# Two of four channel chunks of a 31-tap depthwise convolution computed on TensorE with diagonal weight matrices

## The reference, cut to what matters

```python
def conformer_conv(u, conv_w, conv_b, ln_g, ln_b):
    h = u[..., :D_CONV] * jax.nn.sigmoid(u[..., D_CONV:])            # D_CONV = 512 channels
    h = lax.conv_general_dilated(                                     # depthwise, causal, 31 taps
        h, conv_w[:, None, :], window_strides=(1,), padding=[(CONV_WIDTH - 1, 0)],
        dimension_numbers=("NWC", "WIO", "NWC"), feature_group_count=D_CONV) + conv_b
    return jax.nn.silu(layer_norm(h, ln_g, ln_b))

y_conv = conformer_conv(p[..., :2 * D_CONV], ...)
y_rwkv, v_first = rwkv7_mix(p[..., 2 * D_CONV:], ...)    # a recurrence over the tokens, 8 heads of 64
y = jnp.concatenate([y_conv, y_rwkv], axis=-1) @ w_out
```

## Time and profile before

| | |
|---|---|
| three runs | 1853.69, 1849.98, 1853.31 us; median 1853.31 us |
| the profiled execution, first to last instruction | 1854.3 us (no other time of its own is given) |
| busy: PE / DVE / ACT / POOL | 1675.9 / 1033.2 / 818.9 / 75.5 us |
| mean granted TensorE clock | 0.933 of full speed |
| the stretch of this case | inversion 132.96 to 193.0 us, scan 193.0 to 266.2 us |

### The profile page before, as it was taken

How to read it: one execution, slowest core, us unless ns; L and a number is a source line. 1 busy time by engine, 2 the same in 40 slices (tenths; PEclk the granted TensorE clock), 3 DMA queues, 4 the chain that set the end, 5 groups by cost and what they waited for, 6 DMA issues and landing times.

```text
span 1854.3 us, 29063 instructions
## 1 busy us (share of the span) xinstructions
PE 1675.9 (90%) x11870; PEld 1535.3 (83%) x11870; DVE 1033.2 (56%) x1405; ACT 818.9 (44%) x1211; POOL 75.5 (4%) x84
## 2 busy tenths in 40 slices
PE   6776878997999799999778999999989998899998
PEld 6675657887999699987568999899977998779998
DVE  4868446545554555455855545555443784555554
ACT  5330024545444544444355444544444566554443
POOL 1200000000000000000300000000000004300000
PEclk9887558998999899999899999999989999899999
DMA  6230002523555355544214555455534441145452
GB/s 231 92 115 2 1 23 83 191 104 145 183 183 186 127 187 189 187 162 181 91 69 159 182 181 186 154 187 190 186 118 150 169 182 46 44 162 182 181 183 111
DMA packets 37047, 263.61 MB, mean 142 GB/s; under 512 B 4192, under 2 KB 4320, under 8 KB 5728
## 3 DMA queue, kind: packets, MB, share of 16 engines
q1 hardware_dynamic: 35680, 257.97, 38.4%
q0 software_dynamic: 704, 2.62, 0.4%
q10 hardware_dynamic: 576, 1.78, 0.3%
HBM read 261.30 MB, written 1.05 MB: 141 GB/s over the span
## 4 chain that ended last, share of the span: by engine, by line
PE 83%; DVE 10%; ACT 4%; issue 1%; DMA 1%; POOL 0%; DVEq 0%; POOLq 0%; ACTq 0%
PE PS L374 24%; PE PS L375 24%; PE PS L376 24%; DVE w_lo L1194 2%; PE PS L555 1%; PE PS L368 1%; PE PS L790 1%; DVE arena L1448 1%; PE PS L767 1%; PE PS L456 1%; PE PS L480 1%; DVE x_normed L1211 1%; PE PS L594 1%; DMA x_resid<-x 1%; PE PS L619 1%
## 5 line engine op out<-in xcount | busy, mean ns | idle before, releaser
L1194 DVE TENSOR_TENSOR w_lo<-raw_weights,w_hi 128x1024 fp32r<-128x1024 f32 x488 | 601.9, 1239 | 551.8 <-ACT w_hi L836 551.2
L836 ACT ACTIVATE w_hi<-raw_weights 128x1024 fp32r<-128x1024 f32 x488 | 514.6, 1057 | 579.3 <-PE PS L376 557.1
L374 PE MATMUL PS<-h_hi,w_hi 128*128 128x256 f32 x2320 | 665.0, 287 | 19.8 <-DVE w_lo L1194 13.7
L375 PE MATMUL PS<-h_lo,w_hi 128*128 128x256 f32 x2320 | 662.2, 285 | 0.0
L376 PE MATMUL PS<-h_hi,w_lo 128*128 128x256 f32 x2320 | 661.8, 285 | 0.0
L374 PEld LDWEIGHTS PS<-h_hi,w_hi 128*128 128x128 f32 x2320 | 451.0, 194 | 23.9 <-DVE w_lo L1194 14.3
L375 PEld LDWEIGHTS PS<-h_lo,w_hi 128*128 128x128 f32 x2320 | 450.9, 194 | 2.2 <-issue 0.5
L376 PEld LDWEIGHTS PS<-h_hi,w_lo 128*128 128x128 f32 x2320 | 450.3, 194 | 0.0
L374 PE MATMUL PS<-w_hi,g_hi 128*128 128x512 f32 x440 | 172.0, 391 | 0.0
L375 PE MATMUL PS<-w_lo,g_hi 128*128 128x512 f32 x440 | 171.9, 391 | 0.0
L374 PE MATMUL PS<-w_hi,h_hi 128*128 128x512 f32 x352 | 145.2, 413 | 29.4 <-DVE w_lo L1194 14.5
(11 more groups left out here) (290 smaller groups left out, 1389.7 us busy)
## 6 DMA issues: line engine op xcount, KB each, us to landing
raw_weights<-W SPq DMA_DIRECT2D x244, 1024.0 KB, 4.8
post_gain<-post_gains POOLq DMA_DIRECT2D x3, 512.0 KB, 4.2
x_resid<-x SPq DMA_DIRECT2D x1, 1024.0 KB, 9.4
arena<-mem POOLq DMA_DIRECT2D x1, 1024.0 KB, 5.3
out<-x_resid SPq DMA_DIRECT2D x1, 1024.0 KB, 4.0
ptab<-cols ACTq DMA_DIRECT2D x1, 857.0 KB, 8.7
ctab<-consts ACTq DMA_DIRECT2D x1, 704.0 KB, 5.7
rtab<-rows ACTq DMA_DIRECT2D x1, 176.0 KB, 11.5
```

The costliest lines, as they stand in the source:

```text
L374: mm(out, lhs[0], rhs[0], start=start, stop=False)
L375: mm(out, lhs[0], rhs[1], start=False, stop=False)
L836: A(w_hi[:, n % H, :], raw[:, n % (2 * R), :], ACT.Copy).then_inc(S.hi_ready, 1)
L1194: v.tensor_tensor(w_lo[:, n % H, :], raw[:, n % (2 * R), :], w_hi[:, n % H, :].bitcast(F32), ALU.subtract).then_inc(S.lo_ready, 1)
```

## The change

The convolution's chunks 0 and 1 stay on DVE: `taps` has 62 entries now, and each call of `tap_steps` does half of what it did (4 per half level, 6, 6 and the last 10 in the scan). DVE waits for its own result after every two taps. Chunks 2 and 3 go to PE: a tap is a matmul whose stationary operand is a 128x128 diagonal matrix with the tap's 128 weights and whose moving operand is the shifted `glu`, and all 31 taps of a chunk accumulate in half of PSUM bank 7. The 62 taps are cut into 16 groups of four (the last has two). ACT makes the diagonals, 128x128 each, as identity x weight, into two buffers of four (one in the second half of `conv`, one new). PE takes one group ahead of each of its waits of levels 0 to 3 (four groups a level), and ACT makes the diagonals behind its Q copies. After level 4 ACT moves bank 7 with the bias to `conv`. `conv_ready` now counts two.

```diff
--- before.py
+++ after.py
@@ -143,6 +143,7 @@
         r_f, k_f, v_f = Q_r[:, 0:1024], Q_r[:, 1024:2048], Q_r[:, 2048:3072]
         conv = region(o, 1024); o += 1024
         usig = conv
+        diag = [ap.rearrange("p (s n) -> p s n", s=4) for ap in (conv[:, 512:1024], sb("diagonals", 512)[:])]
         MEM = region(o, 2048).rearrange("p (t d) -> p t d", t=TT)
         glu = region(o, 1024); o += 1024
         decay = region(o, 1024); o += 1024
@@ -225,7 +226,7 @@
                  "consts_loaded sin_ready qk_normed kk_std rows_loaded diff_ready kk_used scan_done "
                  "invP_ready rk_ready g_sum qk_evac qk_sq qk_ms qk_std qk_roped qkT_done qkT_ready v_ready "
                  "ang_ready trig_ready dt_done dt_abs dt_exp dt_ln aneg dta_ready acs_done acs_ready decay2_done "
-                 "conv4_ready xbc_ready z_ready2 sT_done sT_ready g_cb g_lt g_w g_y g_st g_stready g_xdt g_xdec "
+                 "diag_ready conv_mm conv4_ready xbc_ready z_ready2 sT_done sT_ready g_cb g_lt g_w g_y g_st g_stready g_xdt g_xdec "
                  "g_yev ys_sq ys_ms ys_std ysn_ready ysT_done ysT_ready").split()
         S = namedtuple("Signals", NAMES)(*[sem(n) for n in NAMES])
         loaded = [sem(f"loaded{r}") for r in range(R)]
@@ -234,6 +235,9 @@
         def done(eng, name, slot, i=0):
 
             eng.wait_ge(S.half_done, LOOP * i + 2 * (FIRST[name] + slot) + 2)
+
+        PE_TAPS = [(c, back) for c in (2, 3) for back in range(31)]
+        TAP_GROUPS = [PE_TAPS[i:i + 4] for i in range(0, len(PE_TAPS), 4)]
 
         def ffn_half(f, kind, b):
 
@@ -279,7 +283,7 @@
                     pool.wait_ge(S.pin_ready, 11)
                     tt(glu, glu, usig, ALU.mult).then_inc(S.glu_ready, 1)
 
-                    pool.wait_ge(S.conv_ready, 1)
+                    pool.wait_ge(S.conv_ready, 2)
                     pool.wait_ge(S.inv_ready, 12)
                     pool.dma_start(MEM, mem_in.rearrange("(t p) d -> p t d", p=P)).then_inc(S.mem_loaded, 16)
 
@@ -567,11 +571,25 @@
                 gram(6, Bt, Rt, t).then_inc(S.gram_done, 1)
             pe.wait_ge(S.gram_ready, 2)
 
+            def conv_taps(k):
+
+                if k >= len(TAP_GROUPS):
+                    return
+                if k == 0:
+                    pe.wait_ge(S.glu_ready, 1)
+                pe.wait_ge(S.diag_ready, k + 1)
+                for i, (c, back) in enumerate(TAP_GROUPS[k]):
+                    last = mm(PS[:, 7, (c - 2) * T + back:(c - 1) * T], diag[k % 2][:, i, :],
+                              glu[:, c * T:(c + 1) * T - back], start=back == 0, stop=back == 30)
+                last.then_inc(S.conv_mm, 1)
+
             for lv in range(5):
                 for t in range(TT):
+                    conv_taps(4 * lv + t)
                     pe.wait_ge(S.inv_ready, 2 * lv + t + 1)
                     blockmul(3 * t, Loffs[t], XiTs[t], t).then_inc(S.invq_done, 1)
                 for t in range(TT):
+                    conv_taps(4 * lv + 2 + t)
                     pe.wait_ge(S.invq_ready, 2 * lv + t + 1)
                     last = blockmul(3 * t + 1, Xis[t], Qis[t], t)
                     if lv < 4:
@@ -622,7 +640,7 @@
                                   stop=g == 0 or h % 2 == 1)
                 last.then_inc(S.yc_done, 1)
 
-            pe.wait_ge(S.conv_ready, 1)
+            pe.wait_ge(S.conv_ready, 2)
             for t in range(TT):
                 for c in range(4):
                     last = nc.tensor.transpose(PS[:, 4 + t, c * P:(c + 1) * P],
@@ -988,10 +1006,29 @@
 
             act.wait_ge(S.ang_ready, 1)
             A(trig, trig, ACT.Sin).then_inc(S.trig_ready, 1)
+            def diagonals(k):
+
+                if k >= len(TAP_GROUPS):
+                    return
+                if k >= 2:
+                    act.wait_ge(S.conv_mm, k - 1)
+                for i, (c, back) in enumerate(TAP_GROUPS[k]):
+                    last = A(diag[k % 2][:, i, :], ident, ACT.Copy, scale=pc("conv_w", (30 - back) * 4 + c))
+                last.then_inc(S.diag_ready, 1)
+
+            act.wait_ge(S.glu_ready, 1)
+            diagonals(0)
+            diagonals(1)
             for lv in range(5):
                 for t in range(TT):
                     act.wait_ge(S.invq_done, 2 * lv + t + 1)
                     A(Qis[t], PS[:, 3 * t, :], ACT.Copy).then_inc(S.invq_ready, 1)
+                    for k in ((4 * lv + 2,), (4 * lv + 3, 4 * lv + 4, 4 * lv + 5))[t]:
+                        diagonals(k)
+            act.wait_ge(S.conv_mm, len(TAP_GROUPS))
+            for c in (2, 3):
+                last = A(conv[:, c * T:(c + 1) * T], PS[:, 7, (c - 2) * T:(c - 1) * T], ACT.Identity, bias=pc("conv_b", c))
+            last.then_inc(S.conv_ready, 1)
             for g in range(NCK):
                 t, cp = g // 2, 64 * (g % 2)
                 act.wait_ge(S.ru_done, g + 1)
@@ -1431,11 +1468,11 @@
 
             h8 = lambda ap: ap.rearrange("p (h t) -> p h t", h=8)
             b8 = lambda m: m.unsqueeze(1).broadcast_to([P, 8, 64])
-            taps = [(back, c) for back in range(31) for c in range(4)]
+            taps = [(back, c) for back in range(31) for c in range(2)]
 
             def tap_steps(n):
 
-                if len(taps) == 124:
+                if len(taps) == 62:
                     dve.wait_ge(S.glu_ready, 1)
                 for _ in range(min(n, len(taps))):
                     back, c = taps.pop(0)
@@ -1447,7 +1484,7 @@
                         late = conv[:, c * T + back:(c + 1) * T]
                         last_ = v.scalar_tensor_tensor(late, glu[:, c * T:(c + 1) * T - back], weight, late,
                                                        ALU.mult, ALU.add)
-                    if c == 3 and taps:
+                    if c == 1 and taps:
                         step(last_)
                     elif not taps:
                         last_.then_inc(S.conv_ready, 1)
@@ -1479,7 +1516,7 @@
                         v.tensor_tensor(Xi, Xi, PS[:, b + 2, :], ALU.add)
                         last = v.tensor_tensor(h8(Loff), h8(NL), b8(cn("off", (lv + 2) * 64, 64)), ALU.mult)
                     last.then_inc(S.inv_ready, 1)
-                    tap_steps(8)
+                    tap_steps(4)
                     if lv == 0 and t == 0:
 
                         for c in range(4):
@@ -1492,7 +1529,7 @@
                     last = v.scalar_tensor_tensor(Zn[:, g % 2, c, :], PS[:, 3, c * P:(c + 1) * P], Pc[:, c * 4 + g, 64:65],
                                                   cn("pair"), ALU.mult, ALU.mult)
                 last.then_inc(S.z_ready, 1)
-                tap_steps(12 if g < NCK - 2 else len(taps))
+                tap_steps(6 if g < NCK - 2 else len(taps))
 
             y8 = lambda t: Y[:, t, :].rearrange("p (h d) -> p h d", h=8)
             b8h = lambda s_, t: s_[:, 8 * t:8 * t + 8].unsqueeze(2).broadcast_to([P, 8, 64])
```

## The result

| | before | changed kernel |
|---|---|---|
| 13 runs each on the same chip, median | 1853.48 us (1849.98 to 1855.62) | 1857.21 us (1855.17 to 1861.39) |
| profiled execution, span | 1854.3 us | 1856.1 us |
| mean granted clock | 0.933 | 0.941 |

The ratio is 1.0021, with a 95% interval of 1.0013 to 1.0030: slower by 3.7 us, where +2.2 us was forecast. VectorE gave up 62 instructions, TensorE took on 62 matmuls, and the kernel lost a little. Two later executions, one of e2 (2157.61 us) and one of the kernel before (2145.54 us), ran at a mean granted clock of 0.73 and 0.72 and are left out of every median.

A forecast was written before the change was run, and what follows sets the result against it. TensorE carries 83% of the chain, which alternates with VectorE in the inversion; TensorE would bound levels 0 to 3. Scan start +2.9, first scan product -0.9, `w_out` +0.2 on 1853.3 give 1855.5 us, range 1847.5 to 1862.5.

The forecast's parts named there:

- The taps behind t=0: Inversion: VectorE's taps here stand on the path; halving them saves 1.65 us a level, at most 8.2 us over five.
- PE becomes the bound of levels 0 to 3: Inversion: 8.1 us of new TensorE work a level does not fit into 4 us of idle time; VectorE waits.
- 13.5 us a level: TensorE's work in an inversion level: four groups 6.5, eight shape changes 1.6, six block products 5.4 us.
- Full clock from 136.5 on: Inversion: without idle time TensorE's granted clock stays at 1.00 from about 136.5 us, with 1.7 us either way.
- ScalarE hidden: Inversion: the 62 diagonals, at most 1.5 us a group of four, fit ScalarE's idle time and cost nothing.
- The stages: Inversion: VectorE starts later by 4.1 us after level 0, 7.3 after level 3, 4.5 after level 4; scan 2.9.
- The sum: Whole kernel: scan starts 2.9 us later, its first product saves 0.9, `w_out` adds 0.2: 2.2 us over the median.
- The later clock rise in `w_out`: Behind the scan: a later start shifts when the clock rises, a few tenths either way; 0.2 us added.
- Groups in the idle time: Rival, inversion: a group with its changes costs 1.3 instead of 2.0 us, a level 10.8 us; 1846 us, chance 5%.
- dearer groups: Rival, inversion: shape changes of 0.30 us, or late diagonals costing 1 us a level; 1858.5 to 1862 us, chance 12%.
- a half clock in the inversion: Rival: TensorE's clock stays at half there, a level takes 25 us; 1904 us, chance 2%.
- The clock through the scan: Rival: the scan starts and stays at full clock, its matmuls run twice as fast, saving 27 us; 1829 us, chance 8%.

The follow-up runs named there:

- e2: Changed kernel with all 124 taps on VectorE as well as all 16 groups on TensorE, their result thrown away: 1862.51 us, ratio 1.0051.
- e1: Changed kernel without TensorE's groups and ScalarE's diagonals, so half the taps are left out altogether: 1843.56 us, ratio 0.9951.
- e3: Changed kernel with the same 16 groups placed in pairs, four changes of array shape a level instead of eight: 1854.83 us, ratio 1.0008.
- e7: Changed kernel with no ScalarE diagonals behind the second group, all groups using the first two sets: 1856.84 us, ratio 1.0020.
- e11: Kernel before plus four unread full-height 128x256 products ahead of each of the scan's eight waits: 1837.42 us, ratio 0.9919.
- e4: Changed kernel with its groups moved to where TensorE waits: four in gram gaps, two a level, two ahead of the scan: 1840.45 us, ratio 0.9930.
- e6: e4 with all 124 taps kept on VectorE as well, the groups' result thrown away: 1846.79 us, ratio 0.9964.
- e8: e4 plus 16 unread 64x64 products ahead of each of the scan's eight waits for ScalarE: 1820.54 us, ratio 0.9823.
- e12: e8 with 12 instead of 16 unread products per scan wait, plus 64 and 72 ahead of two waits behind the scan: 1821.27 us, ratio 0.9820.
- e9: e4 plus four unread full-height 128x256 products behind each of the scan's eight waits for ScalarE: 1827.14 us, ratio 0.9862.
- e10: e5 with one group moved from the scan into level 4 and one ahead of the scan, six left in it: 1822.40 us, ratio 0.9813.
- e5: e4 with one group a level in levels 0 to 3 and eight groups inside the scan, ahead of its waits: 1820.21 us, ratio 0.9817.

## Why the prediction was right

**The taps behind t=0 were on the path, at most 8.2 us.** Right: e1 gave 9.5 us in the stretch and 10 us in all. The bound "at most" was too low: it left out the clock, whose mean in the stretch went from 0.76 to 0.80.

**PE becomes the bound of levels 0 to 3.** Right, and the best supported step: full PE windows, DVE's waits of 5 us and more, and e2, where twice the work on DVE left the level times unchanged.

**13.5 us a level.** 13.43, 13.60 and 13.33 us. Tap and block product came out as priced; the change of shape was 0.17 us (e3), the prediction took 0.20. In the changed kernel's rows a group with one change takes 151.63 - 149.85 = 1.78 us and a product with one change 152.71 - 151.63 = 1.08 us, which is 1.60 and 0.90 with 0.18 for each change.

**Full clock from 136.5 on.** 1.00 from 135 to 195 us.

**ScalarE hidden.** A group of diagonals takes 1.28 us, and e7 without them is as slow.

**The stages.** From PE's first product of the inversion, the changed kernel's DVE starts are 11.5, 24.9, 38.5, 51.8 and 59.6 us away, before 7.7, 21.0, 32.5, 44.9 and 55.5 us: +3.8, +3.9, +6.0, +6.9 and +4.1 us, and +2.6 at the scan's start. Forecast were +4.1, +4.2, +6.3, +7.3, +4.5 and +2.9, each some 0.3 too high, which is level 0. The scan took 72.2 us to the first transposes behind it (266.68), before 73.1: -0.9, as forecast.

**The sum.** The stretch of the change gave +2.6 - 0.9 = +1.7 us, where the prediction had +2.0. The measured +3.7 us (interval 2.4 to 5.6, so the +2.2 lies just outside it) hold about 2 us more, and these are not in the stretch. The two profiled executions differ by only 1856.1 - 1854.3 = 1.8 us, and their parts are -1.2 us ahead of the inversion (it begins at 132.96 before and at 131.76 here; in e11, which is the kernel before up to the scan, it begins at 131.51, so this is no work of the change), +1.7 us in the stretch and +1.3 us behind it. Every run with both numbers lasts about 1.8 us longer than its span, so the profiled execution of the kernel before stands for about 1856.1 us, 2.6 above the median of 1853.5; the prediction took the 1854.3 for a time and placed it 1.0 us above. The changed kernel's, 1857.88 us, is 0.7 above its median. The pair of profiles therefore can't show where the other 2 us of the medians lie, and no run does. Three of the 13 runs of the changed kernel (1860.18 to 1861.39 us) have a mean granted clock of 0.937 or 0.938 where the other ten have 0.939 to 0.941, so some of it is how the clock fell out.

**The later clock rise in `w_out`.** This term was mis-sized, and its reason was wrong. It was put at 0.2 us, for a later start of `w_out`. In the profiled pair the part behind the scan takes 1.3 us longer, of which 0.6 us lie between the start of `w_out` and the next transposes; there the clock rises at about 285.1 us instead of 283.3. The traces of the kernels whose scan ends at 0.50 show what goes with it:

| kernel | first transposes behind the scan | until the clock rises | from these transposes to the end |
|---|---|---|---|
| e1 | 254.97 | 15.7 us | 1586.7 us |
| e3 | 267.00 | 16.3 us | 1587.3 us |
| before | 266.13 | 17.2 us | 1588.2 us |
| e4 | 250.33 | 17.2 us | 1588.2 us |
| e6 | 257.48 | 17.7 us | 1588.6 us |
| e7 | 266.02 | 18.3 us | 1589.3 us |
| changed | 266.68 | 18.4 us | 1589.4 us |
| e2 | 272.44 | 18.5 us | 1589.4 us |

From there on all eight have the same work. The rest of the kernel follows the moment of the clock's rise almost microsecond for microsecond, and that moment doesn't follow the start: e7 reaches the transposes 0.1 us earlier than the kernel before, and its clock rises 1.1 us later behind them. So the term is worth up to 1.5 us either way from one of these traces to the next. Whether it sits at one value for one kernel is not known, since each was profiled once.

**The rivals.** Groups in the idle time, dearer groups, a half clock in the inversion: none came. The clock through the scan did not hold in this kernel either. But the argument against it was half wrong. "92% busy PE in the scan did not raise it" is true of the scan as it stands, and I laid it to its half-height matmuls. e8 refutes that: with nothing but more half-height products added, the clock holds 1.00. The distance between the two was 32 unread matmuls (e11). The rival's price was near: it has 73 - 27 = 46 us for a scan at full clock, and e12 took 48.1 us with its fillers. That it stayed away was forecast for a reason that does not hold, so there is luck in it.

The Trainium skill, TensorE: Matmul & The Clock Gate, Why this matters for your kernels, asks for bursts without long idle gaps. e8 and e11, with their waits filled, and e9, with short ones, go with it at 1.00. The changed kernel does not: from 200 to 235 us its clock is 0.50 with no gap longer than 0.68 us. Nor does e10, whose clock fell behind one such gap. So the length of the gaps alone doesn't decide. What does was not settled.

## What to carry to other kernels

Before moving work to an engine that "waits 4 us a level", write down its whole order for a level, the new work and its side costs included, and see where the waits lie: here a group went ahead of each of PE's four waits of a level, and only one of the four was a real one, at the product of t=1. The same groups in e4's places were worth 17 us.

If TensorE's clock reads 0.50 in a long serial stretch, try unread matmuls at its waits before anything else: 32 of them gained 16 us (e11). With the taps moved as well, unread matmuls gave 33 us (e8), and useful groups at the same waits gave about 32 us (e5). Size them by a row of the same kernel, so that they end when the wait does.

A change of shape between full-height matmuls and paired corners cost 0.17 us each time here (e3); group the matmuls by shape.

## What the runs showed of the hardware that was not expected

- The granted clock in the scan has two lasting courses for nearly the same work: 0.50 with PE busy 32.95 of 35 us, 1.00 with 53.55 of 59 us (e9), 51.00 of 51 (e8) and 47.00 of 47 (e5).
- It can rise inside the scan: in e5 at about 183.5 us after seven microseconds at 0.50, in e11 at about 196 us after three. PE did not stand still in either stretch.
- One open wait of 0.68 us was followed, 3 us later, by its fall from 1.00 to 0.50 in e10, while e9 ran through eight such waits at 1.00. Two of e10's five runs have the mean clock and the time of an execution without that fall. The scan's own products are the same in both kernels; e9 has a full-height burst of 2.00 us behind each wait, e10's third block one group in place of two.
- Behind the scan eight kernels with the same work differ by up to 2.7 us in the time to the end (1586.7 to 1589.4 us), in step with the moment at which the clock rises in `w_out` (15.7 to 18.5 us behind the transposes).
